# Norms of block 2 by halves of the columns, and rotated parts of latent attention on 64 rows

## The reference

```python
def rms_norm_2(x, g):
    y = xf * lax.rsqrt(jnp.mean(xf * xf, axis=-1, keepdims=True) + EPS)
    return y * g
for layer in range(DEPTH):
    x  = x  + 0.5 * mx[2] * swiglu_2(modulate(rms_norm_2(x,  norm_g[layer, 0]), mx[0], mx[1]), ...)
    xc = xc + 0.5 * mc[2] * swiglu_2(modulate(rms_norm_2(xc, norm_g[layer, 0]), mc[0], mc[1]), ...)
    hx = modulate(rms_norm_2(x,  norm_g[layer, 1]), mx[3], mx[4])
    hc = modulate(rms_norm_2(xc, norm_g[layer, 1]), mc[3], mc[4])
    ...                       # layer 0: latent attention (mla); layer 1: window attention (swa)
    x  = x + 0.5 * mx[8] * swiglu_2(modulate(rms_norm_2(x, norm_g[layer, 2]), mx[6], mx[7]), ...)
    ...                       # the same for xc in layer 0 only
```

```python
d = h @ w_down                         # 512 for q, 256 for kv, 64 for the shared key
s = einsum('bhqd,bhkd->bhqk', qn, kn) + einsum('bhqr,bkr->bhqk', qr, kr)
```

## Time and profile before

| | |
|---|---|
| median of 3 runs | 2797.13 us (2796.72 to 2798.09) |
| profiled execution, its own time | 2795.24 us |
| its span | 2793.5 us |
| TensorE busy | 2671.5 us, 96% |
| VectorE, ScalarE busy | 59%, 40% |
| chain that ended last | PE 92%, DVE 3%, ACT 3% |
| DMA | 403 MB, mean 144 GB/s |

### The profile page before, as it was taken

How to read it: one execution, slowest core, us unless ns; L and a number is a source line. 1 busy time by engine, 2 the same in 40 slices (tenths; PEclk the granted TensorE clock), 3 DMA queues, 4 the chain that set the end, 5 groups by cost and what they waited for, 6 DMA issues and landing times.

```text
span 2793.5 us, 38939 instructions
## 1 busy us (share of the span) xinstructions
PE 2671.5 (96%) x15990; PEld 2331.8 (83%) x15990; DVE 1637.6 (59%) x2673; ACT 1128.5 (40%) x1743; POOL 0.3 (0%) x5
## 2 busy tenths in 40 slices
PE   6999899999989989999989999999989999899998
PEld 6999899999989988888764777888878888777998
DVE  6656777666567765556550546556655444576554
ACT  6465544546544443222242433232232232345443
POOL 0000000000000000000000000000000000000000
PEclk9999999999999999999989999999999999999999
DMA  5543577544356754445512023445534445331454
GB/s 180 182 138 121 168 230 227 170 143 146 113 180 212 231 161 150 144 143 164 160 61 76 3 81 107 149 137 164 159 106 152 142 143 172 115 121 47 164 180 132
DMA packets 114048, 403.27 MB, mean 144 GB/s; under 512 B 12368, under 2 KB 15568, under 8 KB 113744
## 3 DMA queue, kind: packets, MB, share of 16 engines
q1 hardware_dynamic: 113872, 400.79, 44.6%
HBM read 399.69 MB, written 1.05 MB: 143 GB/s over the span
## 4 chain that ended last, share of the span: by engine, by line
PE 92%; DVE 3%; ACT 3%; issue 1%; DMA 0%; SPq 0%; DVEq 0%; ACTq 0%
PE psum L539 27%; PE psum L541 26%; PE psum L540 26%; PE psum L835 2%; PE psum L868 2%; ACT L1086 1%; PE psum L934 1%; PE psum L902 1%; PE psum L915 0%; PE psum L906 0%; PE psum L905 0%; PE psum L889 0%; PE psum L879 0%; DVE arena L1910 0%; DVE wlo L1438 0%
## 5 line engine op out<-in xcount | busy, mean ns | idle before, releaser
L539 PE MATMUL psum<-HHI,whi 128*128 128x256 f32 (+1 forms) x3456 | 1124.9, 325 | 56.6 <-DVE HLO L1504 32.0
L540 PE MATMUL psum<-HLO,whi 128*128 128x256 f32 (+1 forms) x3456 | 1114.7, 323 | 0.0
L541 PE MATMUL psum<-HHI,wlo 128*128 128x256 f32 (+1 forms) x3456 | 1114.1, 322 | 0.0
L1438 DVE TENSOR_TENSOR wlo<-wring,whi 128x1024 fp32r<-128x1024 f32 x590 | 708.4, 1223 | 388.1 <-ACT whi L1056 386.0
L1056 ACT ACTIVATE whi<-wring 128x1024 fp32r<-128x1024 f32 x590 | 607.1, 1054 | 442.0 <-PE psum L541 420.6
L539 PEld LDWEIGHTS psum<-HHI,whi 128*128 128x128 f32 x3456 | 666.5, 193 | 118.1 <-issue 59.9
L540 PEld LDWEIGHTS psum<-HLO,whi 128*128 128x128 f32 x3456 | 666.7, 193 | 49.4 <-issue 1.4
L541 PEld LDWEIGHTS psum<-HHI,wlo 128*128 128x128 f32 x3456 | 665.9, 193 | 48.2
L539 PE MATMUL psum<-HIDHI,whi 128*128 128x256 f32 (+1 forms) x1056 | 357.2, 338 | 0.0
L540 PE MATMUL psum<-HIDLO,whi 128*128 128x256 f32 (+1 forms) x1056 | 357.2, 338 | 0.0
L541 PE MATMUL psum<-HIDHI,wlo 128*128 128x256 f32 (+1 forms) x1056 | 357.1, 338 | 0.0
(11 more groups left out here) (280 smaller groups left out, 1867.9 us busy)
## 6 DMA issues: line engine op xcount, KB each, us to landing
wring<-ffn_in SPq DMA_DIRECT2D x264, 512.0 KB, 4.2
wring<-mod_w SPq DMA_DIRECT2D x144, 512.0 KB, 4.3
wring<-ffn_out SPq DMA_DIRECT2D x96, 448.0 KB, 4.0
wring<-w_proj SPq DMA_DIRECT2D x66, 512.0 KB, 4.2
wring<-w_gate SPq DMA_DIRECT2D x64, 512.0 KB, 3.9
wring<-ffn_out SPq DMA_DIRECT2D x48, 512.0 KB, 4.3
wring<-w_up SPq DMA_DIRECT2D x20, 512.0 KB, 3.4
wring<-w_out SPq DMA_DIRECT2D x16, 512.0 KB, 3.5
```

The costliest lines, as they stand in the source:

```text
L539: mm(out_, w[0], a[0], start=start, stop=False)
L540: mm(out_, w[0], a[1], start=False, stop=False)
L541: return mm(out_, w[1], a[0], start=False, stop=stop)
L1438: TTN(wlo[:, i, :], wring[:, raw_slot(tag, k), :], whi[:, i, :].bitcast(F32), ALU.subtract).then_inc(sem("weights_lo"), 1)
```

## The change

**Norms.** `halved(tag)` is true for (b0, 0), (b1, 0), (b2, 0), (b0, 1) and (b1, 1). Their square sums, factors and scaled tiles are made for 256 columns at a time, with sums and events of their own; `NORMED`, four tiles, takes the place of the 8-tile buffer. At the end of the stage before, the last output tile (ffn) or the last three lots (mlao) are multiplied for the sequence columns first and then for the context columns; behind the first of these context lots TensorE sums the sequence squares. The next stage opens with two lots over the sequence half of all 8 tiles, then over the context half, and the context's sum stands after the third tile. At (b0, 0) the context comes first: its squares, factor and tiles are made inside block 1's last ffn stage (a stage that changes only the sequence half of X), its sum stands behind lot 12, and three lots are opened. ScalarE and VectorE get a written-out order for the tail (`half_tail`). The splits of the stage's last two lots' successors are moved behind the norm.

**Latent attention.** The rotated features of a head are now 64 adjacent rows: two heads on the partitions (QR, QX: four tiles), the key twice (KA as it comes, KR turned). The down projection has 7 lots. The rope uses a matmul with a turn matrix (`turned`, `turn`, as layer 1's attention does). A head's scores are first its four 128-row products, one per query tile, and then the 64-row ones.

```diff
-            order += [("down", 8, 1), ("uq", 6, 0), ("ukv", 4, 0), ("mlao", 8, 1)]
+            order += [("down", 7, 1), ("uq", 6, 0), ("ukv", 4, 0), ("mlao", 8, 1)]
...
+            def half_sum(tag, s_):
+                pe.wait_ge(*bank_free(("ss", tag, s_)))
+                pe.wait_ge(*done("sq_sum", (tag, s_, KT - 1)))
+                mm(bank_of(("ss", tag, s_))[:, 0:SEQ], ones, R[:, seqs(s_)], start=True, stop=True).then_inc(*mark("filled", ("ss", tag, s_)))
...
+            def open_halves(tag, keys, norm):
+                one_, two = halves_of(norm)
...
+                for s_ in (one_, two):
+                    for c in range(KT):
+                        pe.wait_ge(*done("h_ready", (norm, s_, c)))
+                        for j, key in enumerate(keys):
...
+                            last = mm3(bank_of(key)[:, seqs(s_)], (w[0][:, c, :], w[1][:, c, :]),
+                                       (HHI[:, c, seqs(s_)], HLO[:, c, seqs(s_)]), c == 0, c == KT - 1)
...
+                        if s_ == one_ and c == 2:
+                            half_sum(norm, two)
...
+                    if norm == ("b0", 0) and k == 12:
+                        half_sum(norm, 1)
...
+                for s_ in range(2):
+                    tkey = (tag, "o", KT - 1, s_)
+                    pe.wait_ge(*bank_free(tkey))
+                    for k in range(LOTS[tag_out] - tail, LOTS[tag_out]):
...
+                            last = mm3(bank_of(tkey)[:, 0:SEQ], (w[0][:, c - a, :], w[1][:, c - a, :]),
+                                       (hi[:, c, seqs(s_)], lo[:, c, seqs(s_)]), c == 0, c == FT - 1)
+                        if s_:
+                            lot_event(last, tag_out, k)
+                            if k % 3 == 0:
+                                half_sum(norm, 0)
...
+                turned(("tk", 0, 0), ("mla_down", 6), b2["KA"][:, 0, 0:SEQ])
...
+                for i in range(4):
+                    turned(("tm", i), ("mla_qr", i), b2["QR"][:, i, 0:SEQ])
...
                 def scores(h):
+                    p, i = slice(HD * (h % 2), HD * (h % 2) + HD), h // 2
+                    KA, KR = b2["KA"][p, 0, :], b2["KR"][p, 0, :]
+                    for qt in range(4):
...
+                        if qt < 2:
+                            mm(bank, b2["QN"][:, h, q], b2["KN"][:, h, :], start=True, stop=False)
+                        else:
+                            mm(bank[:, 0:CTX], b2["QN"][:, h, q], b2["KN"][:, h, SEQ:BOTH], start=True, stop=False)
+                    for qt in range(4):
...
+                        if qt < 2:
+                            mm(bank[:, 0:SEQ], b2["QX"][p, i, q], KR, start=False, stop=False)
+                        mm(ctx_part, b2["QR"][p, i, q], KA[:, SEQ:BOTH], start=False, stop=True).then_inc(*mark("filled", ("ms", h, qt)))
...
+            def half_tail(tag, lots_, tiles_, norm):        # ScalarE
...
+                for t in tiles_:
+                    act.wait_ge(*done("half_ready", (tag, t)))
+                    square_half(norm, 0, t)
+                split_ahead(tag, lots_[0])
+                half_factor(norm, 0)
+                half_hi(norm, 0, range(2), l, n3)
...
+                half_hi(norm, 0, range(2, 3), l, n3)
+                act.wait_ge(*done("x_ready", (tag, tiles_[-1])))
+                square_half(norm, 1, tiles_[-1])
+                half_hi(norm, 0, range(3, KT), l, n3)
+                half_factor(norm, 1)
+                half_hi(norm, 1, range(KT), l, n3)
+                for k in lots_[1:]:
+                    split_ahead(tag, k)
...
+            def half_tail(tag, lots_, keys, norm, coef, l_in):   # VectorE, s: scaled, r: low part
...
+                split_ahead(tag, lots_[0])
+                v.wait_ge(*done("factor", (norm, 0)))
...
+                s(0)
+                s(1)
+                r(0)
+                s(2)
+                r(1)
+                for m, key in zip(tiles_[:-1], keys):
+                    second(m, key)
+                s(3)
+                r(2)
+                second(tiles_[-1], keys[-1])
+                s(4)
+                r(3)
+                for m in tiles_:
+                    add_square_half(norm, 1, m)
+                for k in range(5, KT):
+                    s(k)
+                    r(k - 1)
+                r(KT - 1)
+                half_norm(norm, 1, l, n3)
```

More of the change, by code:

```diff
@@ L576, in dense, with dense_behind, ffn @@
                     dense_lot(tag, k, n, h)
-            def ffn(tag_in, tag_out, tag, n):
-                dense(tag_in, n, h_of(tag), lambda c: done("h_ready", (tag, c)))
+            def dense_behind(tag, norm):
+                first = 3 if norm == ("b0", 0) else 2
+                open_halves(tag, [(tag, k) for k in range(first)], norm)
+                for k in range(first, LOTS[tag]):
+                    dense_lot(tag, k, BOTH, (HHI, HLO))
+            def ffn(tag_in, tag_out, tag, n, norm):
+                if halved(tag):
+                    dense_behind(tag_in, tag)
+                else:
+                    dense(tag_in, n, h_of(tag), lambda c: done("h_ready", (tag, c)))
                 hi, lo, _ = hid_of(tag)
-                for k in range(LOTS[tag_out]):
+                tail = 3 if n == BOTH and halved(norm) else 0
+                for k in range(LOTS[tag_out] - tail):
                     pe.wait_ge(*lo_ready(tag_out, k))
@@ L851, in mla_pe @@
             def mla_pe():
-                dense("down", BOTH, (HHI, HLO), lambda c: done("h_ready", (("b1", 0), c)))
+                dense_behind("down", ("b1", 0))
                 pe.wait_ge(*done("mla_sq", 5))
@@ L1099, in ffn @@
                 logarithm_table()
-                for k in range(3 * KT):
+                tail = 3 if n == BOTH and halved(norm) else 0
+                for k in range(3 * KT - tail):
                     if k < 3 * KT - 1:
@@ L1785, in residual @@
                 ln(v.memset(R[:, 0:n], 0.0))
-                for k in range(KT):
+                tail = 3 if halved(norm) else 0
+                for k in range(KT - tail):
                     v.wait_ge(*lot_done(tag, k))
@@ L1815, in ffn @@
                 ln(v.memset(R[:, 0:norm_n], 0.0))
-                for k in range(3 * KT):
+                if norm == ("b0", 0):
+                    v.wait_ge(*done("ctx_loaded", 0))
+                tail = 3 if n == BOTH and halved(norm) else 0
+                for k in range(3 * KT - tail):
                     m, bkey = k // 3, (tag, "o", k // 3)
@@ L2066 @@
     uq_cols = np.concatenate([h * 192 + ar(P) for h in range(8)]
[L2067 removed]
+                              + [h * 192 + P + ar(HD) for h in range(8)])
     ukv = g["mla_w_ukv_2"][0]
```

238 lines of the change are left out of this document (170 added, 68 removed).

## The result

The changed kernel takes 2760.06 us (median of 4 runs, 2758.10 to 2761.86), the one before 2797.61 beside it: ratio 0.9866, interval 0.9853 to 0.9878, or 37.5 us less. The forecast was 2757 (2745 to 2771). The profiled execution has a span of 2758.5 against 2793.5.

What follows compares the result with a forecast made beforehand. TensorE, busy 96% of the span and carrying 92% of the last-ending chain, was taken as the bound. Norms 20.0 plus attention 20.4 gave 40.4 us, taking the median from 2797.1 to 2757, range 2745 to 2771.

Steps and rivals of the forecast that it cites:

- attention without its lot: Latent attention: 17.4 us left after waits, less 0.7 for the key's turn and 1.7 for the queries' turns.
- TensorE runs on behind the stage before, one stop per site in the middle of opening, two table loads in its chain: Halved norms except b0,0: first half's chain hidden, second half uncovered, its two loads of about 1.28 us within a 3.2 us stop.
- The second sum waits 0.8, at b2,0 2.2: Opening lots: TensorE waits for the other half's squares, 0.8 us, or 2.2 at b2,0, which has three tiles in halves.
- The low clock costs 2.2 per site: Halved norms except b0,0: after the idle stop TensorE falls to the lower clock, losing 2.2 us each.
- b0,0 has no clock loss and a stop of 1.5: At b0,0: cost 4.0 us, 1.5 of it from the third opened lot's late low part; nothing stands still for long.
- A 64-row matmul takes what a 128-row one does: Latent attention scores: 0.43 us per 256-wide matmul saves 2.58 per head, 20.6 over 8; at 0.54, 5 less.
- Waits in attention: Latent attention: head 0 waits 2.1 instead of 1.3, clock loss 1.0 on average, four mid-loop weight splits about 1.4 us.
- The fit of 0.15 us: Latent attention: softmax weights come at 7.15 and 8.7 us, TensorE wants them at 7.75 and 8.85, so they fit.
- The table switch: Uncovered halves: 1.28 us per load; with the skill's 1.38 drain 2.8 longer each, 2768; dearer seams, this included, chance 0.15.
- softmax: Rival in latent attention: last weights 1.5 us late in every head, losing 12 us, 2769; chance 0.13.
- the heads kept clock 1.00: Judges the rival that latent attention falls to 1.2 GHz, 8 heads costing 73 us more, 2829; chance 0.04.
- The halves hide their first factor: Judges the rival that ScalarE makes it only after TensorE's second half, norms gaining nothing, 2777; chance 0.05.

Runs made afterwards that it cites:

- mla_only: The kernel before with only the attention's part of the change, all norms whole: 2781.79 us, ratio 0.9945 to the kernel before.
- norms_only: The kernel before with only the halved norms, attention and eight lots of down as before: 2779.46 us, ratio 0.9941 to the kernel before.
- experiment 3: Against the changed kernel, the context's squares at b0,0 are summed and normalised earlier: 2758.02 us; with the sum two lots later, 2755.33 us in a single run.
- experiment 2: Against the changed kernel, rotated products padded to 128 rows: 2758.56 us; or 64-row products interleaved, eight row-count changes per head instead of two: 2765.54 us, one run.
- pad128: The changed kernel with the latent attention's rotated products on all 128 rows, the other head's rows zero: 2758.56 us, ratio 0.9868 to the kernel before.

## Why the prediction was right, step by step

The stages' lengths in the two profiled executions give each term (TensorE's first matmul of a stage to the next stage's first). The down projection's gain is split: the lot is 24 x 0.227, the rest is b1,0's. Against neighbours that differ in the attention's part alone the projection is 5.7 shorter (before and mla_only) and 5.4 (norms_only and the changed kernel).

| term | forecast | measured |
|---|---|---|
| b0,0 | 7.0 | 4.4 |
| b1,0 | 4.3 | 4.0 |
| b2,0 | 2.3 | 1.6 |
| b0,1 and b1,1 | 2.7 and 3.7 | 2.7 and 3.6 |
| attention without its lot | 15.0 | 14.4 |
| the eighth lot of down | 5.4 | 5.45 (worked out) |
| sum | 40.4 | 36.2 |

The sum is 4.2 us under the forecast, and the medians' 37.5 is 2.9 under it; the spans of the two profiled executions differ by 35.0.

- *TensorE runs on behind the stage before, one stop per site in the middle of opening, two table loads in its chain:* right, four times, 3.4 us where 3.2 was worked out (2.9 at b2,0).
- *The second sum waits 0.8, at b2,0 2.2:* 1.08 and 2.13.
- *The low clock costs 2.2 per site:* it stood at three of the four sites, about 1.7 each, and also at b0,0. It depends on more than the stop: behind equal stops of 3.4 it came at b1,0 and not at b2,0. There the missing clock loss hid other costs: the longer stop, 0.7 for a weight's low part and 0.2 at the first tile. The gain was still 0.7 under the forecast.
- *b0,0 has no clock loss and a stop of 1.5:* the line that is off most, 2.6 us. The stop was 2.41, the clock fell behind it (1.7), and the context's sum waited 0.93 instead of 0.7. The forecast saw that the third lot's low part would be late "behind the half norm's steps", but sized it too small; experiment 3 shows these steps to be the cause, and that the two stages are 4.7 us shorter when they stand earlier.
- *A 64-row matmul takes what a 128-row one does:* right by itself (experiment 2). The forecast, though, bounded only the matmul and not the passage from one kind to the other: 8 x 0.39 = 3.1 us less than the 20.6. It is the largest single term that was missed. The kernel before had shown it, and shown also that its 0.54 for 8-row matmuls was the clock: the same 16 records in layer 0, at full clock, take 228.67 - 225.03 = 3.64 us, eight times 0.43 and 0.2 for a half change at either end.
- *Waits in attention:* overestimated, which nearly made up for that. That the attention's term came out at 14.4 for 15.0 is luck: two errors of 3.1 and 2.5 us against each other. Head 0 waits 1.74 (2.1 forecast) and no clock loss followed, the four mid-loop splits cost 0.7 (one head of 10.15) instead of 1.4, the key's turn 0.3 instead of 0.7. The fit of 0.15 us held: only that one head still waits for its weights, in the changed kernel and in pad128, whose heads take the 9.07 us that the fit was worked out for.
- *The table switch:* Exp starts 0.01 us behind the load's end, at 1404.56, in the uncovered half as well. The 1.38 us of drain of the Trainium skill ("ScalarE: Activation LUTs", What ACT_TABLE_LOAD costs) do not show. By that page the stop would have been some 6.2 us long (an estimate: 3.4 and twice 1.38).
- *Rivals:* softmax didn't take over, and the heads kept clock 1.00, their transposes and 64-row products included. The halves hide their first factor at the old stage's end (no stop there at the three ffn sites, 0.17 us at b2,0), but not wholly: with the short factor the second sum's pause falls from 1.08 to 0.2.

The executions' other stages differ too, without a cause in the change: block 1 is 3.2 us longer after, since the low clock behind the 8-row matmuls of layer 0 came only there, and the window attention's stage 2.6 us shorter (107.66 and 110.31 us, at a mean clock of 0.97 and 0.94).

## What to carry to other kernels

Cutting a serial chain in two hid nearly all of its first part here and left the second part's own length as the stop: shorten what stands in that part (here two table loads) before or together with the cut, and each gains from the other. Before crediting a wait to the work named in it, shorten that work once; the stop before the query products ignored its factor's length, and a step that only stood first in line was the cause. Matmuls on fewer rows cost no more by themselves, but keep them together or pad them: each change between row counts had its price. Before calling a term a guess, look through the other stages of the trace: the price of this one stood in the window attention.

## What the runs showed of the hardware that was not expected

- A change between 128-row and 64-row fp32 matmuls costs about 0.2 us (0.195 and 0.196 from two and eight changes per head).
- Two 64-row fp32 matmuls of 256 columns on different halves of the rows, one behind the other and into different banks, take the time of one: four in 1.07 us in the window attention, a change's 0.2 included.
- A reciprocal of 128x256 on VectorE takes 1.74 us and one of 128x512 3.35, some four and five times another VectorE operation of that size (0.42 to 0.48, and 0.69 for an addition); one of 128x1 takes 0.16.
- The inverse square root of 128x256 on ScalarE is 0.46 us, a plain activation, when its table is loaded.
- The lower clock is not tied to one cause: behind equal stops of 3.4 us it came at three norms and not at a fourth, and behind the same 8-row matmuls of layer 0 it came in the changed kernel and not in the one before.
- Kernels that do the same in a stage differ there by 1.3 to 1.7 us or a multiple through the clock alone, more than several of the edits here are worth: the window attention's stage is 107.66, 109.33 and 110.58 us long in the changed kernel, norms_only and mla_only, at a mean clock of 0.97, 0.95 and 0.94.
